# Weighted value sums of two heads in one block of native fp32 matmuls, in column tiles of one bank

## The reference, cut to what matters

```python
s = jnp.einsum('bhqd,bhkd->bhqk', q_blk, k).astype(jnp.float32) * scale
s = jnp.where(k_pos[None, :] <= q_pos[:, None], s, NEG_INF)
p = jax.nn.softmax(s, axis=-1).astype(v.dtype)
return jnp.einsum('bhqk,bhkd->bhqd', p, v)
...
h = h + rms_norm(mix @ w_out[l], attn_post_g[l])
```

## Time and profile before

| | us |
|---|---|
| median of 3 executions | 596.29 |
| lowest and highest | 593.0, 596.85 |
| the profiled execution | 595.35 |
| its span | 593.5 |
| attention from the first probability transposes on | about 115 to 213 in the span |

### The profile page before, as it was taken

How to read it: one execution, slowest core, us unless ns; L and a number is a source line. 1 busy time by engine, 2 the same in 40 slices (tenths; PEclk the granted TensorE clock), 3 DMA queues, 4 the chain that set the end, 5 groups by cost and what they waited for, 6 DMA issues and landing times.

```text
span 593.5 us, 8348 instructions
## 1 busy us (share of the span) xinstructions
PE 576.1 (97%) x2900; PEld 484.7 (82%) x2900; DVE 412.0 (69%) x787; ACT 309.7 (52%) x651; POOL 105.7 (18%) x165
## 2 busy tenths in 40 slices
PE   7999999989999999999999999999979999999995
PEld 7988898878777788898888888888868888888884
DVE  3449573688888605536766757759658889877897
ACT  5563171689799605445344353355235666655552
POOL 1163210345689401220000000000000001000004
PEclk9999999999999999999999999999989999999999
DMA  8441522000220064036688777867897554565503
GB/s 302 132 141 54 173 76 72 1 1 2 72 73 0 2 227 163 1 114 238 230 300 282 252 254 278 296 232 270 313 374 281 213 191 163 214 211 169 189 0 141
DMA packets 43489, 99.35 MB, mean 167 GB/s; under 512 B 3905, under 2 KB 22081, under 8 KB 39617
## 3 DMA queue, kind: packets, MB, share of 16 engines
q1 hardware_dynamic: 42416, 98.94, 47.4%
q10 hardware_dynamic: 1040, 0.00, 0.1%
HBM read 81.11 MB, written 17.83 MB: 167 GB/s over the span
## 4 chain that ended last, share of the span: by engine, by line
PE 72%; DMA 16%; DVE 4%; ACT 2%; issue 2%; SPq 2%; DVEq 0%; POOLq 0%; POOL 0%; ACTq 0%
PE bank L1210 23%; PE bank L1211 22%; PE bank L1212 22%; DMA pair_sums<-stage 14%; PE bank L1380 2%; DMA w_raw<-in_w_down 2%; DVE pT_lo L804 1%; ACT probs L624 1%; DMA x_sb<-in_x 1%; DVE bank L936 1%; ACT w_hi L512 1%; PE bank L1317 1%; SPq L343 1%; PE bank L1216 1%; PE bank L1249 1%
## 5 line engine op out<-in xcount | busy, mean ns | idle before, releaser
L1210 PE MATMUL bank<-uT_hi,w_hi 128*128 128x512 f32 (+1 forms) x280 | 104.1, 372 | 0.0
L1211 PE MATMUL bank<-uT_lo,w_hi 128*128 128x512 f32 (+1 forms) x280 | 103.8, 371 | 0.0
L1212 PE MATMUL bank<-uT_hi,w_lo 128*128 128x512 f32 (+1 forms) x280 | 103.8, 371 | 0.0
L512 ACT ACTIVATE w_hi<-w_raw 128x1024 fp32r<-128x1024 f32 (+2 forms) x65 | 62.6, 1008 | 77.0 <-PE bank L1212 64.8
L804 DVE TENSOR_TENSOR w_lo<-w_raw,w_hi 128x1024 fp32r<-128x1024 f32 (+1 forms) x57 | 67.8, 1230 | 34.6 <-ACT w_hi L512 34.5
L1210 PE MATMUL bank<-w_hi,a_hi 128*128 128x512 f32 x224 | 88.0, 393 | 3.0 <-DVE w_lo L804 3.0
L1211 PE MATMUL bank<-w_lo,a_hi 128*128 128x512 f32 x224 | 87.9, 392 | 0.0
L1212 PE MATMUL bank<-w_hi,a_lo 128*128 128x512 f32 x224 | 87.7, 392 | 0.0
L807 DVE SCALAR_TENSOR_TENSOR w_lo<-w_raw,g_up,w_hi 128x256 fp32r<-128x256 f32 x128 | 52.0, 479 | 50.8 <-ACT w_hi L512 50.8
L512 ACT ACTIVATE w_hi<-w_raw,g_up 128x256 fp32r<-128x256 f32 x128 | 52.9, 496 | 48.2 <-PE bank L1212 30.7
L1210 PE MATMUL bank<-w_hi,uT_hi 128*128 128x512 f32 (+1 forms) x160 | 61.9, 387 | 0.0
(11 more groups left out here) (149 smaller groups left out, 1042.3 us busy)
## 6 DMA issues: line engine op xcount, KB each, us to landing
w_raw<-in_w_up SPq DMA_DIRECT2D x16, 1024.0 KB, 8.1
stage<-in_w_down SPq DMA_DIRECT2D x15, 1024.0 KB, 4.9
pair_sums<-stage SPq DMA_DIRECT2D x15, 1024.0 KB, 9.8
w_raw<-pair_sums SPq DMA_DIRECT2D x15, 1024.0 KB, 4.8
w_raw<-in_w_down SPq DMA_DIRECT2D x13, 1024.0 KB, 7.0
w_raw<-in_w_in SPq DMA_DIRECT2D x6, 1024.0 KB, 6.0
w_raw<-in_w_out SPq DMA_DIRECT2D x4, 1024.0 KB, 4.8
x_sb<-in_x SPq DMA_DIRECT2D x8, 256.0 KB, 6.0
```

The costliest lines, as they stand in the source:

```text
L512: return nc.scalar.activation(out, whole, ACT.Copy, scale=scale)
L1210: nc.tensor.matmul(out, lh, rh, start=start, stop=False)
L1211: nc.tensor.matmul(out, lh, rl, start=False, stop=False)
L1212: return nc.tensor.matmul(out, ll, rh, start=False, stop=stop)
```

## The change

The weighted sums of heads 2m and 2m + 1 become one block. Values and transposed probabilities are no longer split: v_sb and four buffers pT hold plain fp32, and the product is a plain fp32 matmul. An even head writes partitions 0 to 63 of bank 6, an odd one 64 to 127, with the matmuls of the two heads alternating. Bank 3 of the transposed probabilities is copied by ScalarE alone and banks 4 and 5 by VectorE alone. The blocks stand at odd i from 3 to 17. Bank 6 is emptied once per pair, with 128 partitions. OUT_PIECES gives one piece to each iteration from 4 to 15 and two to 16 and 17.

```diff
-        v_hi = sb("v_hi", [P, 2, NT, HW], F32R, stack=att)
-        v_lo = sb("v_lo", [P, 2, NT, HW], F32R, stack=att)
+        v_sb = sb("v_sb", [P, 2, NT, HW], stack=att)
...
-        pT_hi = [sb(f"pT_hi{i}", [P, TRI], F32R, stack=att) for i in range(2)]
-        pT_lo = [sb(f"pT_lo{i}", [P, TRI], F32R, stack=att) for i in range(2)]
+        pT = [sb(f"pT{i}", [P, TRI], stack=att) for i in range(4)]
...
-        OUT_PIECES = {i: [i - 4] if i < HEADS else [2 * i - 12, 2 * i - 11] for i in range(4, 14)}
+        OUT_PIECES = {**{i: [i - 4] for i in range(4, NH)}, NH: [12, 13], NH + 1: [14, 15]}
...
-            sp.wait_ge(o_full, NH)
+            sp.wait_ge(o_full, NH // 2)
...
             def p_part(i):
-                if i >= 2:
-                    act.wait_ge(o_full, i - 1)
-                for n, (b, c, w) in enumerate(PT_COPY):
-                    act.wait_ge(pT_full, 3 * i + n + 1)
-                    hi_part(pT_hi[i % 2][:, c:c + w], ps[b][:, 0:w]).then_inc(ph, 1)
...
+                if i >= 4:
+                    act.wait_ge(o_full, (i - 4) // 2 + 1)
+                b, c, w = PT_COPY[0]
+                act.wait_ge(pT_full, 3 * i + 1)
+                nc.scalar.copy(pT[i % 4][:, c:c + w], ps[b][:, 0:w]).then_inc(p3_ready, 1)
+
+            def o_part(m):
+                act.wait_ge(o_full, m + 1)
+                hi_part(uT_hi[:, m, :], ps[6][:, :]).then_inc(oh, 1)
...
-            for t in range(NT):
-                dve.wait_ge(vh, t + 1)
-                lo_part(v_lo[:, 0, t, :], ps[t][:, :], v_hi[:, 0, t, :]).then_inc(vl, 1)
...
             def p_part(i):
-                for n, (b, c, w) in enumerate(PT_COPY):
-                    dve.wait_ge(ph, 3 * i + n + 1)
-                    lo_part(pT_lo[i % 2][:, c:c + w], ps[b][:, 0:w], pT_hi[i % 2][:, c:c + w]).then_inc(pl, 1)
...
+                if i >= 4:
+                    dve.wait_ge(o_full, (i - 4) // 2 + 1)
+                for n, (b, c, w) in enumerate(PT_COPY[1:]):
+                    dve.wait_ge(pT_full, 3 * i + n + 2)
+                    nc.vector.tensor_copy(pT[i % 4][:, c:c + w], ps[b][:, 0:w]).then_inc(p45_ready, 1)
...
                     elif i >= 3:
-                        pe.wait_ge(pl, 3 * (i - 3) + 1)
+                        pe.wait_ge(p3_ready, i - 2)
...
-                        pe.wait_ge(pl, 3 * (i - 1) + k + 1)
+                        pe.wait_ge(*((p45_ready, 2 * (i - 1) + k) if k else (p3_ready, i)))
...
-            def weighted(i):
-
-                pe.wait_ge(pl, 3 * (i + 1))
-                if i >= 1:
-                    pe.wait_ge(ol, i)
-                g, vc = i // HEADS, slice(VD * (i % HEADS), VD * (i % HEADS) + VD)
+            def weighted(m):
+
+                pe.wait_ge(p3_ready, 2 * m + 2)
+                pe.wait_ge(p45_ready, 4 * m + 4)
+                if m >= 1:
+                    pe.wait_ge(ol, m)
                 for k in range(NT):
                     w = slice(PT_OFF[k], PT_OFF[k] + P * (NT - k))
-                    out_k, stop = ps[6][:, P * k:TOP], k == NT - 1
-                    last = mm3(out_k[0:VD], v_hi[:, g, k, vc], v_lo[:, g, k, vc], pT_hi[i % 2][:, w], pT_lo[i % 2][:, w], k == 0, stop)
+                    for i in (2 * m, 2 * m + 1):
+                        r0, vc = VD * (i % 2), slice(VD * (i % HEADS), VD * (i % HEADS) + VD)
+                        last = nc.tensor.matmul(ps[6][r0:r0 + VD, P * k:TOP], v_sb[:, i // HEADS, k, vc], pT[i % 4][:, w],
+                                                start=k == 0, stop=k == NT - 1)
                 last.then_inc(o_full, 1)
...
-                if i >= 3:
-                    weighted(i - 2)
+                if i >= 3 and i % 2:
+                    weighted(i // 2 - 1)
                 k_prep(3 if i == 1 else i + 3)
-                if i == 1:
-                    weighted(0)
```

More of the change, by code:

```diff
@@ L193, in build @@
         qup, qup_c, q_roped = sem("qup"), sem("qup_c"), sem("q_roped")
-        v_full, vh, vl = sem("v_full"), sem("vh"), sem("vl")
+        v_full, v_ready = sem("v_full"), sem("v_ready")
         qT_full, qh, ql = sem("qT_full"), sem("qh"), sem("ql")
@@ L198, in build @@
         s_ri, s_norm = sem("s_ri"), sem("s_norm")
-        pT_full, ph, pl = sem("pT_full"), sem("ph"), sem("pl")
+        pT_full, p3_ready, p45_ready = sem("pT_full"), sem("p3_ready"), sem("p45_ready")
         o_full, oh, ol = sem("o_full"), sem("oh"), sem("ol")
@@ L467, in out_piece @@
                     last.then_inc(wo_ready, 1)
-            for i in range(NH):
+            for i in range(NH + 3):
                 for n in OUT_PIECES.get(i - 1, []):
                     out_piece(n)
-                for n, t in enumerate(S_ORDER):
+                for n, t in enumerate(S_ORDER if i < NH else []):
                     pool.wait_ge(s_ri, 2 * i + (1 if n == 0 else 2))
@@ L595, in _ @@
                 act.wait_ge(v_full, t + 1)
-                hi_part(v_hi[:, 0, t, :], ps[t][:, :]).then_inc(vh, 1)
+                hi_part(v_sb[:, 0, t, :], ps[t][:, :]).then_inc(v_ready, 1)
             in_hi(7)
@@ L659, in _ @@
                 act.wait_ge(proj, 3 * NT + t + 1)
-                hi_part(v_hi[:, 1, t, :], ps[4 + t][:, :], stat[:, 0, t, 3:4]).then_inc(vh, 1)
+                hi_part(v_sb[:, 1, t, :], ps[4 + t][:, :], stat[:, 0, t, 3:4]).then_inc(v_ready, 1)
             p_part(0)
@@ L676, in _ @@
                     exps(i + 1, S_ORDER[1:n])
-                if i >= 2:
-                    o_part(i - 2)
+                if i >= 3 and i % 2:
+                    o_part(i // 2 - 1)
                 if i + 1 < NH:
@@ L962, in p_part, with o_part @@
             def p_part(i):
-                for n, (b, c, w) in enumerate(PT_COPY):
-                    dve.wait_ge(ph, 3 * i + n + 1)
-                    lo_part(pT_lo[i % 2][:, c:c + w], ps[b][:, 0:w], pT_hi[i % 2][:, c:c + w]).then_inc(pl, 1)
[L967 to L970, removed]
+                if i >= 4:
[3 more added lines that the diff above has]
+                    nc.vector.tensor_copy(pT[i % 4][:, c:c + w], ps[b][:, 0:w]).then_inc(p45_ready, 1)
+            def o_part(m):
+                dve.wait_ge(oh, m + 1)
+                lo_part(uT_lo[:, m, :], ps[6][:, :], uT_hi[:, m, :]).then_inc(ol, 1)
             for i in (0, 1):
@@ L982, in _ @@
                     k_part(2)
-                dve.wait_ge(vh, NT + t + 1)
-                lo_scaled(v_lo[:, 1, t, :], ps[4 + t][:, :], stat[:, 0, t, 3:4], v_hi[:, 1, t, :]).then_inc(vl, 1)
             inverse_sums(1)
@@ L1307, in q_prep @@
                     if i == 0:
-                        pe.wait_ge(vl, NT)
+                        pe.wait_ge(v_ready, NT)
                         pe.wait_ge(q_roped, NT)
                     elif i >= 3:
-                        pe.wait_ge(pl, 3 * (i - 3) + 1)
+                        pe.wait_ge(p3_ready, i - 2)
                     if i == HEADS:
@@ L1323, in k_prep @@
                     if i in (2, 3):
-                        pe.wait_ge(vl, NT + i + 1)
+                        pe.wait_ge(v_ready, NT + i + 1)
                     elif i > 3:
@@ L1375, in probs_T @@
                     if i == 0 and k == 0:
-                        pe.wait_ge(vl, NT + 2)
+                        pe.wait_ge(v_ready, NT + 2)
                     if i >= 1 and k < 3:
-                        pe.wait_ge(pl, 3 * (i - 1) + k + 1)
+                        pe.wait_ge(*((p45_ready, 2 * (i - 1) + k) if k else (p3_ready, i)))
                     for t in range(k, NT):
@@ L1413, in out_early @@
                 pe.wait_ge(s_exp, NT * NH)
-                pe.wait_ge(ol, 4 * (c + 1))
+                pe.wait_ge(ol, 2 * (c + 1))
                 out_tile(0, c)
@@ L1439, in _ @@
                     if c == 0 and t == NT - 1:
-                        pe.wait_ge(ol, NH)
+                        pe.wait_ge(ol, NH // 2)
                     last = out_tile(t, c)
```

## The result

The changed kernel took 603.08 us in the median of 20 runs (595.29 to 611.47), the kernel before 595.59 in 20 runs beside it (591.83 to 597.96). The comparison of the two gives a ratio of 1.0085, 95% interval 1.0058 to 1.0112: slower, by about the 1% that can just be told from no change. The forecast was 594.8 us and no change; the range, 587.0 to 613.5, holds the time.

What follows compares the result with a forecast made beforehand. The prediction took TensorE, 97% busy at full clock, to bound the kernel. Odd iterations +4.6 us and even ones -5.1 gave -0.5 on 595.35, so 594.8 us and no measurable change; range 587 to 613.5.

Steps and rivals of the forecast that it cites:

- Part 1, the block: Attention's value sums: sixteen blocks of 12 matmuls become eight of 8, two heads side by side, 2.37 us each.
- X: Time of the new two-head block of value sums: between 1.04 and 4.74 us, taken as 2.37.
- The two rivals that priced a worse overlap: Head halves in turn: 4.74 us a block, 613.8 us, chance 0.22; overlap only at joints: 3.56, 604.3 us, 0.14.
- the one with a transpose's price: Rival: native fp32 value sums cost what fp32 transposes cost, 1.13 us a block, 584.9 us in all; chance 0.14.
- Part 1, the odd iterations: Attention iterations holding the new block: each grows by 0.57 us against the old 1.80 us block, eight by 4.6 us.
- Part 3: Work leaving the other engines, some 1 us a head on VectorE and ScalarE, and moved output weight pieces: counted as nothing.
- Part 2, the even iterations: Seven even attention iterations (4 to 16) lose their 1.80 us block but bare the waits it covered: 5.1 us off together.
- Block 0's move: First head's value block leaves i = 1, where it ran inside a wait ending at 121.56: gains nothing there.
- The sum: Whole kernel: +4.6 us for odd iterations, -5.1 for even ones, so -0.5 us on 595.35, giving 594.8.
- two halves that run in turn: Rival: the two heads' column halves in the value block do not overlap, 4.74 us, 613.8 us in all; chance 0.22.
- the q chain: Before the probability transposes: q transposes, ScalarE's qT_hi, VectorE's qT_lo; bared in iterations 8, 10, 12, gain 0.43 us each.
- the 0.35 that stood on "slower": Chance of a slower kernel: 0.22 halves in turn, 0.10 overlap only at joints, 0.03 the forecast's own share.

Runs made afterwards that it cites:

- e2: Changed kernel with the native fp32 value sums of one head in every iteration, the first head's at i = 1: 601.71 us, ratio 1.0093 to before.
- e5: Changed kernel with 182 unused bf16 matmuls put only where its TensorE stood idle in attention: 595.09 us, ratio 0.997 to before.
- e6: Changed kernel with the output weight pieces spread over the iterations as in the kernel before: 602.92 us, ratio 1.0105 to before.
- e9: Changed kernel with fewer unused matmuls than e5, so that about 1.0 us of each gap stays idle: 595.88 us, ratio 0.9988 to before.
- e4: Changed kernel with each two-head block cut in two, k = 0 at odd i, the rest in the even iteration behind: 589.93 us, ratio 0.9882 to before.

## Why the prediction was right and where it failed

- *Part 1, the block.* X = 2.37, measured 2.31 us, with both heads side by side (e2: 2.29 for one). The two rivals that priced a worse overlap, with 0.36 of the chances, and the one with a transpose's price are refuted.
- *Part 1, the odd iterations.* "Grows by 0.57 us": measured at full clock +0.50 in iteration 3, +0.52 in 7, and only +0.17 in 9 and 11 (6.11 instead of 5.94 and 5.93). Over the seven from 3 to 15 it is 1.9 us, not 4.0. In iteration 9 of before, TensorE stood for ScalarE's exponentials in the middle of the scores (the row below). In e5 it doesn't, and the scores of that iteration take 2.09 us (164.21 to 166.30) instead of 2.50 (165.01 to 167.51). This is relief of the other engines, of which Part 3 said "I count none".

```profile
166.45 0.18 PEld L1210 LDWEIGHTS bank<-kT_hi,qT_hi 64*128 64x128 f32 x1 [0.33 <-ACT probs L624]
```

- *Part 2, the even iterations.* Gains of 0.8 in 4 and 6 were 0.84 and 0.95 us, of 0.43 in 8, 10 and 12 were 0.36, 0.38 and 0.36, of 0.43 in 14 was 0.79, of 1.8 in 16 was 1.8 (the output tile starts 1.01 us behind the transposes in e5, 2.82 before). The idle time ahead of the transposes was 1.46 us for a forecast of 1.5 or so, 1.72 in one.
- *Part 3.* The output pieces cost nothing (e6). Block 0's move was counted at nothing because the wait "ended at 121.56 anyway". The wait did end there, at 121.39; but with block 0 in it TensorE was idle 0.87 us, and without it 2.59, and behind that the clock fell in 2 of 6 profiled executions, for 1.6 and 1.3 us.
- *The sum.* It said -0.5 us. The trace less its falls gives a span of 593.1 for 593.5, and e5 595.09 us beside 597.08 for before, -2.0. The near agreement is in part luck: the odd iterations cost 2 us less than the sum has, and about a microsecond of that is returned at the turn to the down weights, where TensorE waits 3.00 us for w_lo in before and 3.7 to 5.1 in the faster kernels.
- *The range.* It holds 603.08, by luck: its upper part stood there for two halves that run in turn.

The step that failed is that the clock was taken as a constant: "What bounds the kernel now" reads, rightly for attention before the change, that TensorE "was granted its full speed", and Part 2 prices the new idle time as if that would stay. Part 2 saw rightly that the block's cover was taken from the q chain and that "TensorE stands idle 1.7 us there", and priced the idle time at its own length. In place of that the runs show idle gaps of 1.46 to 2.59 us, ahead of iterations 2, 7, 9, 11 and 13, behind four of which TensorE ran at 1.2 GHz for up to one iteration in the profiled execution; a fall in it cost 1.6 to 4.8 us, up to three times the gap, 12.4 us in all, and the two medians lie 7.5 us apart. This was a rival with no place in the list. Nearly all of the 0.35 that stood on "slower" was for causes that did not occur.

The Trainium skill describes a case near to this: "TensorE: Matmul & The Clock Gate", A second HAM failure mode: psum-queue depth-cycling, tells of a kernel in which frequent short idle times between groups of matmuls let the clock swing between half and full and lower the throughput at an unchanged median time per matmul. The traces agree that the clock swings: behind 1.72 us idle the block of iteration 7 took 4.47 us, behind 1.46 us idle that of iteration 9 took 2.31. The cause of the idle time is another here, the q chain.

## What to carry to other kernels

Where TensorE is the limit, a gap laid bare in its stream isn't free even if the sum of busy times says so: look at the granted clock by stretch, and at its spread over runs, before and after. Work that does not fit beside a wait is better spread than gathered: the same eight matmuls, cut into two parts of 1.0 and 1.5 us, were 15 us faster by the medians (603.08 and 588.15) than in one of 2.3. With e5's 595.09 between them, about half of that is idle time filled and half the clock. Before restructuring, a few unused matmuls in the gap tell whether the clock is what one is losing, provided that they lie inside the wait, and not behind it. And a gap in the trace of before that has a fall behind it, wherever it stands, says what a new gap may cost.

## What the runs showed of the hardware

- Native fp32 matmuls with 64 output columns each, on the two column halves in turn, ran side by side without loss: 2.31 us for two heads of 1280 columns, 2.29 for one.
- The granted clock of one core's TensorE fell to 0.50 within microseconds of an idle time of 1.46 or 1.72 us in 8 of 16 cases, and came back to 1.00 in the same iteration or at its end; with seven waits of 0.85 to 1.06 us (e9) it stayed at 1.00 in attention.
- The fp32 transposes of the probabilities (ten in 1.04 us at full clock, 2.02 at half in e4 from 121.86 on) and the blocks (2.31 and 4.47) slow down alike when it falls. The copies of VectorE and ScalarE don't (688 and 587 ns in the mean over the changed kernel's attention, 690 and 587 in e5, which has no fall there), so that a fall is seen as a busy TensorE with the others idle.
